# Attention by groups: two heads and one branch a step, with probabilities scaled by GpSimd and outputs summed in PSUM

## The reference

```
p_c = masked_softmax(q @ k_cmp.T * scale, cmask)   # 31 compressed blocks
o_c = p_c @ v_cmp
o_s = masked_softmax(q @ ks.T * scale, causal) @ vs   # selected blocks
o_w = masked_softmax(q @ kw.T * scale, causal) @ vw   # sliding window
o = o_c * gates[..., 0] + o_s * gates[..., 1] + o_w * gates[..., 2]
out = o.reshape(B, S, H * dk) @ w_out
```

## Time and profile before

| | |
|---|---|
| Median of 3 runs | 1523.6 us (1522.2 to 1524.91) |
| The profiled execution | 1524.09 us, span 1522.3 us |
| Mean granted clock of TensorE | 0.991 of full |
| TensorE busy | 1468.9 us (96% of the span) |
| VectorE, ScalarE, GpSimd busy | 718.9, 716.8, 677.4 us (47%, 47%, 44%) |
| Four groups of layer 1's attention | from about 756 to 1047.4 us of the span |

### The profile page before, as it was taken

The page is one execution under the profiler, slowest core; times in us unless marked ns, Lnnn a source line. Parts: engine busy times, 40 slices in busy tenths (PEclk is TensorE's granted clock), DMA queues, the critical chain, the costliest instruction groups (busy, mean ns, idle before and its releaser), DMA issues.

```text
span 1522.3 us, 23455 instructions
## 1 busy us (share of the span) xinstructions
PE 1468.9 (96%) x7566; PEld 1221.6 (80%) x7566; DVE 718.9 (47%) x1256; ACT 716.8 (47%) x1305; POOL 677.4 (44%) x970
## 2 busy tenths in 40 slices
PE   6999978999999999999999999999999999999998
PEld 5877757888888888877978787878888888888886
DVE  5477772643434300246466767674644444410053
ACT  5245543654444423357365656464744444423262
POOL 4634434365656555364420202111465656555452
PEclk9999998999999999999999999999999999999999
DMA  5321111223232333242510101010132222332221
GB/s 201 121 70 56 55 42 56 94 100 106 87 106 87 106 102 97 70 135 84 167 44 15 56 1 55 14 41 21 66 136 96 96 96 96 96 97 98 97 97 56
DMA packets 37131, 126.22 MB, mean 83 GB/s; under 512 B 6096, under 2 KB 6864, under 8 KB 36816
## 3 DMA queue, kind: packets, MB, share of 16 engines
q1 hardware_dynamic: 31824, 115.88, 22.9%
q10 hardware_dynamic: 5248, 9.55, 1.8%
HBM read 123.32 MB, written 2.10 MB: 82 GB/s over the span
## 4 chain that ended last, share of the span: by engine, by line
PE 58%; issue 17%; POOL 16%; DVE 5%; ACT 4%; POOLq 0%; ACTq 0%; DVEq 0%
PE banks_a L1204 22%; POOL w_lo L297 15%; PE banks_b L1213 9%; PE banks_a L1213 8%; PE banks_a L1576 4%; PE banks_b L1204 4%; PE banks_a L1181 4%; PE banks_b L1548 2%; PE banks_b L1368 2%; DVE nm L940 1%; PE banks_a L1387 1%; PE banks_a L1467 1%; ACT w_hi L358 1%; ACT y L361 1%; PE banks_b L1551 0%
## 5 line engine op out<-in xcount | busy, mean ns | idle before, releaser
L297 POOL TENSOR_TENSOR w_lo<-w_raw,w_hi 128x256 fp32r<-128x256 f32 x852 | 648.0, 793 | 767.0 <-ACT w_hi L358 766.9
L358 ACT ACTIVATE w_hi<-w_raw 128x1024 fp32r<-128x1024 f32 x213 | 225.6, 1061 | 284.1 <-PE banks_b L1213 137.5
L1204 PE MATMUL banks_a<-nT_hi,w_hi 128*128 128x512 f32 (+1 forms) x968 | 344.5, 377 | 0.0
L1204 PE MATMUL banks_a<-nT_lo,w_hi 128*128 128x512 f32 (+1 forms) x968 | 342.7, 375 | 0.0
L1204 PE MATMUL banks_a<-nT_hi,w_lo 128*128 128x512 f32 (+1 forms) x968 | 342.2, 375 | 0.0
L1204 PEld LDWEIGHTS banks_a<-nT_hi,w_hi 128*128 128x128 f32 x968 | 174.6, 190 | 32.0
L1204 PEld LDWEIGHTS banks_a<-nT_hi,w_lo 128*128 128x128 f32 x968 | 173.7, 189 | 32.1
L1204 PEld LDWEIGHTS banks_a<-nT_lo,w_hi 128*128 128x128 f32 x968 | 173.8, 189 | 31.3
L846 DVE SCALAR_TENSOR_TENSOR y<-banks_a,conv,y 128x511 f32<-128x511 f32 x88 | 66.0, 750 | 218.2 <-ACT y L459 217.6
L459 ACT ACTIVATE y<-banks_a,conv 128x512 f32<-128x512 f32 x88 | 68.6, 780 | 207.6 <-PE banks_a L1204 207.5
L940 DVE TENSOR_REDUCE nm<-banks_b 128x2 f32<-128x256 f32 (+2 forms) x96 | 79.2, 825 | 27.1 <-PE banks_b L1371 14.5
(11 more groups left out here) (256 smaller groups left out, 2400.6 us busy)
## 6 DMA issues: line engine op xcount, KB each, us to landing
w_raw<-in_w SPq DMA_DIRECT2D x213, 512.0 KB, 3.3
g_pre<-in_gains ACTq DMA_DIRECT2D x6, 512.0 KB, 5.1
x<-in_x SPq DMA_DIRECT2D x4, 512.0 KB, 9.6
g_post<-in_gains ACTq DMA_DIRECT2D x4, 512.0 KB, 7.6
out<-x SPq DMA_DIRECT2D x4, 512.0 KB, 2.6
pe_raw<-in_pT ACTq DMA_DIRECT2D x2, 512.0 KB, 6.0
w1k<-in_w ACTq DMA_DIRECT2D x1, 1024.0 KB, 4.9
w1v<-in_w ACTq DMA_DIRECT2D x1, 1024.0 KB, 6.9
```

What stands on the lines that cost most here:

```text
L297: pool.tensor_tensor(w_lo[slot][:, cols], w_raw[k % RAW][:, cols], w_hi[slot][:, cols].bitcast(F32), ALU.subtract).then_inc(S["w_lo_done"], 1)
L358: act.activation(w_hi[u % RING][:, :], w_raw[u % RAW][:, :], ACT.Copy).then_inc(S["w_hi_done"], 1)
L1204: m = pe.matmul(bank[:, cols], w[:, k * P:(k + 1) * P], r[:, k, cols], start=(k, pas) == (0, 0), stop=(k, pas) == (KT - 1, 2))
```

## The change

A step becomes (pair of heads m, branch c, query tile k): two heads of one branch. Their probabilities are multiplied in place by gate / row sum before they are turned. `inverse_sums` (VectorE) takes maximum and reciprocal of the row sums of a step; `weigh` (GpSimd) does two products, one for each head, each with two factors that differ by row. The values are held as TensorE's weights (64 columns: `Vg[:, kb, side(c)]`), and the turned probabilities move (128 columns); so the output is born turned, [64 features of a head, tokens], the first head on partitions 0 to 63 and the second on 64 to 127 of bank A[m]. `cvalues` starts the sum there, and both branches add to it. Gone are `weights_of_branches`, `read_branches`, `add_branches`, `blocks_out` and `gturn_o`. `oT1_hi` and `oT1_lo` are read from A[m]: pair 0 within the loop (after step 9), pair 1 in the next lead-in. The compressed probabilities are multiplied by gate / sum on VectorE before `cturn`. `gp` has three buffers (`DEEP`), and the lists work three steps ahead. ScalarE issues `gexps(1)` before its copies of `pcT` and `Vg`. GpSimd's `low` for the fourth unit is split into quarters between `weigh` of steps 3 to 6. The lists of TensorE and GpSimd are written out for all four groups, where TensorE's was a loop in hardware over three.

```diff
+DEEP = 3
-            ("gp", [P, 2, 2, SEQ], F32), ("gpT", [P, 2, 2, SEQ], F32),
+            ("gp", [P, DEEP, 2, SEQ], F32), ("gpT", [P, 2, 2, SEQ], F32),
+        sequence = [(m, c, k) for m in range(2) for c in range(2) for k in range(TT)]
  # GpSimd
+            def weigh(g, n):
+                pool.wait_ge(S["gstat_done"], 16 * g + n + 1)
+                for j in range(2):
+                    cols = gp[:, n % DEEP, j, 0:width]
+                    gate = gates[:, qt, bass.ds(12 * g + (3 * (2 * m + j) + 1 + c), 1)]
+                    pool.tensor_scalar(cols, cols, grec[:, n % 4, j:j + 1], gate, ALU.mult, ALU.mult)\
+                        .then_inc(S["gnorm_done"], 1)
+            def group(g, i):
+                for k in range(3):
+                    low(UG + k, (UG + k) % RING, UG + 4 * i + (k + 1))
+                for n in range(len(sequence)):
+                    weigh(g, n)
+                    if 3 <= n < 3 + PARTS:
+                        low(UG + 3, (UG + 3) % RING, UG + 4 * i + 4, (n - 3,))
  # ScalarE, group
-                gexps(*seq[0])
+                gexps(0)
...
+                gexps(1)
                 act.wait_ge(S["cpT_done"], g + 1)
...
+                gexps(2)
+                for n in range(len(sequence)):
+                    gp_turned(n)
+                    if n + DEEP < len(sequence):
+                        gexps(n + DEEP)
                     if n == 1:
                         w_high(u + 3, i, per)
+                    if n == 9:
+                        goT_high(2 * g, 0)
  # VectorE, group
+                def inverse_sums(n):
+                    dve.wait_ge(S["gprobs_done"], 32 * g + (2 * n + 2))
+                    link(dve.tensor_scalar(grec[:, n % 4, :], gsum[:, n % 4, :], 1e-30, None, ALU.max))
+                    signal(dve.reciprocal(grec[:, n % 4, :], grec[:, n % 4, :]), "gstat_done", 16 * g + n + 1)
...
+                signal(dve.tensor_tensor(pc[:, :, :, :].rearrange(flat), pc[:, :, :, :].rearrange(flat),
+                                         cst[:, 2, :].unsqueeze(2).broadcast_to([P, TT * GHEADS, N_PAD]), ALU.mult),
+                       "cp_done", g + 1)
+                inverse_sums(0)
+                gmaxima(1)
+                inverse_sums(1)
+                gmaxima(2)
+                for n in range(len(sequence)):
+                    gp_turned(n)
+                    if n + DEEP - 1 < len(sequence):
+                        inverse_sums(n + DEEP - 1)
+                    if n + DEEP < len(sequence):
+                        gmaxima(n + DEEP)
+                    if n == 9:
+                        goT_low(2 * g, 0)
  # TensorE, group
+                    pe.matmul(A[m], Vblk[:, bass.ds(g, 1), 2 * HEAD * m:2 * HEAD * m + 2 * HEAD]
+                              .rearrange("p a n -> p (a n)"), pcT[:, :, :].rearrange("p t n -> p (t n)"), start=True,
+                              stop=False)
+                    for kb in range(qt + 1):
+                        for j in range(2):
+                            ins = pe.matmul(A[m][side(j), tok(qt)], Vg[:, kb, side(c)],
+                                            gpT[:, n % 2, j, kb * P:(kb + 1) * P], start=False,
+                                            stop=c == 1 and k == TT - 1 and kb == qt)
...
                 cturn()
                 vturn()
                 cvalues(0)
+                cvalues(1)
+                gscores(2)
+                for n in range(len(sequence)):
+                    gturn(n)
+                    if n + DEEP < len(sequence):
+                        gscores(n + DEEP)
                     if n:
+                        gvalues(n - 1)
+                gvalues(len(sequence) - 1)
```

More of the change, by code:

```diff
@@ L338, in _ @@
             o_normed(DIFF_HEADS - 1)
-            lows(ahead + 2 * (DIFF_HEADS - 2), UNITS)
+            UG = PLAN["group"] + RING
+            lows(ahead + 2 * (DIFF_HEADS - 2), UG)
+            def weigh(g, n):
+                m, c, k = sequence[n]
+                qt = ORDER[k]
+                width = (qt + 1) * P
+                pool.wait_ge(S["gstat_done"], 16 * g + n + 1)
[11 more added lines that the diff above has]
+                        low(UG + 3, (UG + 3) % RING, UG + 4 * i + 4, (n - 3,))
+            for g in range(GROUPS):
+                group(g, g)
+            lows(UG + 4 * GROUPS, UNITS)
         @block.scalar
@@ L686, in gexps @@
-                def gexps(h, k):
+                def gexps(n):
+                    m, c, k = sequence[n]
                     qt = ORDER[k]
[L688 to L696, removed]
@@ L1162, in _ @@
+                inverse_sums(0)
[10 more added lines that the diff above has]
+                        goT_low(2 * g, 0)
             group(0, True)
-            with chain.loop(1, GROUPS, 3 * 3 + 4 + 1 + 1 + 2 + TT + 4 * 4) as g:
+            with chain.loop(1, GROUPS, 3 * 3 + 4 + 1 + 3 + 1 + 4 * TT) as g:
@@ L1164, in _ @@
                 group(g, False)
[L1165 to L1166 removed]
+            goT_low(2 * GROUPS - 1, 1)
             output_norm(2, 3, "out1", 8, 4)
@@ L1530, in cvalues, with gturn @@
+                def gturn(n):
+                    pe.wait_ge(S["gnorm_done"], 32 * g + 2 * n + 2)
+                    if n:
+                        pe.wait_ge(S["gpTa_done"], 16 * g + n)
+                        pe.wait_ge(S["gpTv_done"], 16 * g + n)
                     else:
                         pe.wait_ge(S["vg_done"], g + 1)
-                    for t in range(2):
-                        mm = pe.matmul(A[1 - m][:, 256 * t:256 * t + 256], pcT[:, 2 * m + t, :],
-                                       Vblk[:, bass.ds(g, 1), :].rearrange("p a n -> p (a n)"), start=True, stop=True)
@@ L1554, in gturn @@
-                def gturn(h, k):
-                    pe.wait_ge(S["gprobs_done"], 2 * step(h, k) + 2)
-                    if not (first and h == 0 and k == 0):
-                        pe.wait_ge(S["gpTa_done"], step(h, k))
-                        pe.wait_ge(S["gpTv_done"], step(h, k))
-                    for c in range(2):
-                        for kb in range(ORDER[k] + 1):
-                            m = transpose(A[2 + c][:, kb * P:(kb + 1) * P], gp[:, k % 2, c, kb * P:(kb + 1) * P])
-                        m.then_inc(S["gT_done"], 1)
@@ L1586, in group @@
                         compressed_kv()
-                    if n == 0 and not first:
-                        pe.wait_ge(S["opair_done"], 4 * g)
-                        for m in range(2):
-                            gturn_o(m)
                     if n == 2:
```

242 lines of the change are left out of this document (81 added, 161 removed).

## The result

The changed kernel takes 1562.51 us (median of 4 runs, 1561.34 to 1564.53) against 1522.92 for the kernel before in the same runs: a ratio of 1.0256, 95% interval 1.0243 to 1.0269, so 39.6 us slower. The prediction said 1554, with a range of 1538 to 1578. The profiled execution has a span of 1560.9 us, against 1522.3.

A forecast was written before the change was run, and what follows sets the result against it. It took VectorE and ScalarE waiting for each other to bind the loop: 6.6 us a group, 26.4 in four, plus 4.0 for TensorE's clock, on 1524.1 gave 1554.5, stated as 1554 (range 1538 to 1578).

The forecast's parts named there:

- The ring: In the loop, VectorE's maxima and `inverse_sums` and ScalarE's exponentials wait for each other: 2.70 us a step, 10.8 for four.
- Pair 0 after step 9: After step 9, ScalarE's high half, VectorE's low half and a later copy make inverse(12) come 1.85 us later.
- The start: At the loop's start, VectorE's added product delays `cturn` and ScalarE's later `pcT` copy delays `cvalues`, by some 4 us.
- Two heads overlap: In TensorE's values, heads on different halves of the array's columns overlap: 1.2 us for 16 records, 1.9 to 2.1 otherwise.
- The term of 8.8 us for four steps: TensorE's loop work for four steps with overlapping heads: 5.3 us of turns and scores plus 3.5 of values.
- TensorE bound: Rival, chance 0.27: heads do not overlap, TensorE needs 11.1 us for four loop steps; 9.8 us a group, 1569 with clock.
- GpSimd's products: GpSimd's scaling of probabilities: 1.04 us for 512 columns, 0.83 for 384, hidden in the loop except at its end.
- The clock: TensorE's lower clock after idle time at the loop's start: 1.0 us a group, bounds 0 and 1.7, 4.0 in all.
- the end: From inverse(15) to the group's end, GpSimd's products, turn(15) and the last values: 4.2 us in all.
- No change: Rival, chance 0.04: the start's delay is absorbed and both sides of the loop balance near 10.3 us for four steps.
- faster: Rival, chance 0.07: TensorE alone binds the loop, with overlapping heads; 5.9 us a group less, 1500.

The follow-up runs named there:

- e1_order: Changed kernel with VectorE's maxima of the next step issued before the reciprocal of this step's sums in the loop: 1538.93 us, ratio 1.0103 to the kernel before.
- e3_pair0: Changed kernel with pair 0's output halves made in the next group's lead-in instead of after step 9: 1555.86 us, ratio 1.0216 to the kernel before.
- e2_copies: Changed kernel with ScalarE's copies of `pcT` and `Vg` put before the exponentials of step 1: 1549.81 us, ratio 1.0161 to the kernel before.
- e9: Changed kernel with both heads' values written to one half of the array's columns, except a pair's last step: 1565.36 us, ratio 1.0277 to the kernel before.
- e10: e4_all3 with both heads' values written to one half of the array's columns, except a pair's last step: 1534.06 us, ratio 1.0070 to the kernel before.
- e4_all3: Changed kernel with the edits of e1_order, e2_copies and e3_pair0 together: 1518.35 us, ratio 0.9969 to the kernel before.
- e6: Changed kernel with GpSimd's products cut to 16 columns of each row: 1562.85 us, ratio 1.0251 to the kernel before.
- e7_warm: Changed kernel with matmuls nothing reads in TensorE's idle time, 5 before `cturn` and 12 before `cvalues`: 1555.12 us, ratio 1.0201 to the kernel before.
- e12: e4_all3 with step 2's scores and maxima moved ahead at the loop's start and 5 unread matmuls before `cturn`: 1513.72 us, ratio 0.9933 to the kernel before.
- e8: e4_all3 with each step's values issued head by head instead of alternating between heads: 1523.41 us, ratio 1.0002 to the kernel before.

## Why the prediction came out as it did

The sign, the mechanism and the range held; the time was 8.5 us too low (30.4 us of loss forecast, 39.6 measured). By its own steps:

- **The ring.** 2.70 us a step, 10.8 for four, was predicted; 11.07 and 10.67 were measured, and inverse(2) to inverse(15) took 37.5 us against 36.95 (thirteen steps and pair 0). e1_order, which changes the order of the two entries and nothing else, opens it. The prediction said what stays when it is gone: TensorE.
- **Pair 0 after step 9**: 1.85 us predicted (the terms named for it add up to 1.91); in the trace step 12 comes 2.2 us late, and e3_pair0 gives back 1.7 a group.
- **The start.** Counted from the group's first projection, `cturn` was predicted at 28.5 us and came at 28.6 (869.58 - 840.96); `cvalues` at 32.6 and came at 32.75. e2_copies gives back 3.2 a group, the clock's share included.
- **Two heads overlap**: 1.2 us predicted for 16 records, 1.15 measured, and e9 and e10 show that it goes when both heads use one half of the columns. The term of 8.8 us for four steps was 8.7 (e4_all3). The rule that I weighed against it, in the Trainium skill ("TensorEngine Tiling (Array Packing)", Key Properties), that a change of tiling mode drains the array, shows in bursts of four: they take 0.44 us in e4_all3, where a quarter of the 1.03 of its bursts of 16 is 0.26. A part that stays when the burst gets short is what a drain at each change would leave, so the trace agrees so far; but the overlap gives back more.
- **TensorE bound** (0.27): would have needed 11.1 us for four steps. It didn't come; e10 shows the price of missing overlap once the ring is open, 15.7 us.
- **GpSimd's products**: the size was off. 1.04 and 0.83 us for 512 and 384 columns were predicted, 0.77 and 0.67 measured. In groups 0 and 1 it changed nothing, since turn(15) is held by TensorE; in groups 2 and 3, from the sums of step 15 to the end, the sum was 0.3 us too long. The Trainium skill's figure ("GPSIMD Engine Reference", Elementwise — side-by-side cycle accounting; the prediction names the section Engine selection for it) gave an estimate of 0.33 for 384; the measurement lies above it, since 0.35 us is paid whatever the width: from 0.452 to 0.773 over 384 more columns is 0.84 ns a column, and the products of 16 columns in e6 take 0.357.
- **The clock is the term that was mis-sized.** I took 1.0 us a group within bounds of 0 and 1.7. I had foreseen one stretch; there are two. At the start, the compressed product took 3.44 us instead of 1.98. What that costs is read against e7_warm, where it doesn't happen: inverse(2) starts 37.3 us after the first projection in groups 1 to 3 of that run, and at 38.7, 39.6 and 39.6 in the changed kernel, so 1.4, 2.3 and 2.3 us. (The prediction's 37.9 is where inverse(2) ends; without the clock it would have ended at 37.7, so the rest of the start was right.) At the end of groups 0 and 1, turn(14) waits 1.8 us (ScalarE copies step 13 only after the exponentials of step 15), the clock falls, and turn(14) and the values of step 13 take 2.93 us, where 0.38 and 1.15 at the full clock make 1.5: 1.4 lost, on the path, since turn(15) stands behind them. In groups 2 and 3 turn(13) runs at half clock instead, and the sums of step 15 come 0.8 us later. From these terms the clock cost an estimated 2.8 us in group 1 and at most 3.1 in groups 2 and 3. Predicted without clock, a group has 79.0 us; measured were 82.4, 81.9 and 81.9, so 3.1 over. Of the rest, 0.3 to 0.6 lies between inverse(2) and inverse(15), most of it in pair 0, and the end, priced too high, gives some of it back. By 2.1 a group more than I had put down, the sum is at the 1562 of the result. Some luck is in this: group 0 lost 11.5 us, 1.8 more than the other three on average, and what lies outside the groups is 1.9 us shorter in the profile. I had predicted neither, and they cancel.
- **No change and faster** had 0.11 together. The faster one becomes true once the three orders are mended (e4, e12), though it gives 1.6 to 2.4 us a group and not 5.9: `cturn` still waits 1.3 us, turn(1) 1.6, and two turns in four steps another 0.9.

One thing stays open: what the stretch at the group's end costs by itself. No run removed it alone. The groups of the changed kernel bound it: from the sums of step 15 to the end of the group it is 6.2 us in group 1, with the stretch there, and 4.3 in group 2, where it came earlier and had delayed these sums by 0.8; so moving it was worth 1.1 us.

## What to carry to other kernels

When work moves to other engines, write down each engine's list and look for an instruction that waits for what the next instruction of the same list must start: busy shares of 45% said nothing, and swapping two entries was worth 23.6 us. The third buffer of `gp` had not opened the ring. And count what a wait before TensorE does to the work behind it: an idle 1.8 to 3 us was paid a second time at half clock, in a place where TensorE was not even the bound. An experiment that gives TensorE more to do can hide its own price in this way, as e9_same_half did.

## What was not expected of the hardware

- Two heads issued one after the other, head by head, overlap for a part: 16 records took 1.51 us, against 1.15 in turns (1.03 in e4) and 1.89 in one half. In e8's trace bursts of 8 and 4 lose nothing by the order. How far ahead a matmul of the other half can start was not measured by itself.
- After idle times of 1.31 and 3.03 us with 1.1 us of work between them, the granted clock was 0.51 over 3.4 us, and after one of 1.78 us it was 0.50: the lower of the two levels, 1.2 of 2.4 GHz (windows above). The same kernel had this second stretch at another place in groups 2 and 3. Seventeen matmuls that nothing reads removed the first and left the second; in e1, e4 and e9, where TensorE waits 0.9 to 1.2 us before turn(14), the end of every group ran at the full clock.
- A GpSimd product by two factors per row costs 0.35 us and 0.84 ns a column (0.45 to 0.77 us for 128 to 512 columns), less per column than its product of two tensors in the earlier trace rows.
